# The first weight chunk loaded behind the first x tile, and its products mixed with the turns of the later tiles

## What is computed

```
z = x @ w_in                       # 1152 x 1024 by 1024 x 6216; columns: q, k, v, qi, ki, wi, xr, gr, ga, gb
q, k, qi, ki = rope(...)           # rotary position on the heads
attn = sparse_attention(...)       # an indexer (qi, ki, wi) picks the keys of each query, then softmax
rnn  = RG-LRU(conv(xr)) * gelu(gr) # needs softplus(-lru_lambda), gate biases, conv weights: "the vectors"
x = LayerNorm1(alpha * x + (sigmoid(ga) * (attn @ w_a) + sigmoid(gb) * (rnn @ w_r)) @ w_out)
x = LayerNorm2(alpha * x + HierMoE(x))
```

## Time and profile before

| | |
|---|---|
| median of 3 runs | 1666.08 us (1664.17 to 1671.99) |
| the profiled execution, its own time | 1661.35 us |
| its span | 1659.5 us |
| mean granted TensorE clock | 0.956 of full speed |
| busy in the span: TensorE / VectorE / ScalarE / GpSimd | 1496.0 / 876.7 / 531.9 / 434.4 us |

### The profile page before, as it was taken

The page is one execution under the profiler, slowest core; times in us unless marked ns, Lnnn a source line. Parts: engine busy times, 40 slices in busy tenths (PEclk is TensorE's granted clock), DMA queues, the critical chain, the costliest instruction groups (busy, mean ns, idle before and its releaser), DMA issues.

```text
span 1659.5 us, 24972 instructions
## 1 busy us (share of the span) xinstructions
PE 1496.0 (90%) x10014; PEld 1344.0 (81%) x10014; DVE 876.7 (53%) x1648; ACT 531.9 (32%) x960; POOL 434.4 (26%) x465
## 2 busy tenths in 40 slices
PE   5989999999999899899999998999994299999990
PEld 5976679899999567789899897999994288888880
DVE  4025827999996577431546465443265034434445
ACT  4224542211111565520465655011011022222225
POOL 0744534813233000013334343231100302111110
PEclk7999999999999899999999999999998599999995
DMA  5111010232232830853111111244015768888946
GB/s 190 37 30 29 26 45 16 66 114 82 81 105 72 247 87 25 314 178 91 35 46 42 45 36 47 88 170 150 30 77 200 277 209 228 247 249 277 265 120 247
DMA packets 138089, 204.08 MB, mean 123 GB/s; under 512 B 14676, under 2 KB 89396, under 8 KB 137984
## 3 DMA queue, kind: packets, MB, share of 16 engines
q1 hardware_dynamic: 131808, 180.53, 33.6%
q0 software_dynamic: 6176, 22.10, 5.6%
HBM read 143.99 MB, written 58.61 MB: 122 GB/s over the span
## 4 chain that ended last, share of the span: by engine, by line
PE 76%; DMA 10%; DVE 5%; POOL 4%; issue 2%; ACT 2%; SPq 1%; POOLq 0%; DVEq 0%; ACTq 0%
PE psum L544 18%; PE psum L546 17%; PE psum L545 17%; DMA w_gate_up<-in_w_gate_up 5%; PE psum L1326 5%; PE psum L1140 3%; DMA x_and_experts_by_token<-expert_out,row_token 2%; PE psum L1130 2%; PE psum L1009 2%; PE psum L1162 2%; PE psum L1111 2%; POOL x_by_expert L935 1%; PE psum L1278 1%; PE psum L1318 1%; POOL roped L899 1%
## 5 line engine op out<-in xcount | busy, mean ns | idle before, releaser
L544 PE MATMUL psum<-x_hi,ring_hi 128*128 128x384 f32 x768 | 259.0, 337 | 0.5 <-ACT v L1518 0.5
L546 PE MATMUL psum<-x_lo,ring_hi 128*128 128x384 f32 x768 | 256.6, 334 | 0.0
L545 PE MATMUL psum<-x_hi,ring_lo 128*128 128x384 f32 x768 | 256.5, 334 | 0.0
L905 POOL CAST ring_hi<-ring_raw 128x512 fp32r<-128x512 f32 x88 | 67.1, 763 | 582.3 <-PE psum L546 415.8
L1326 PE MATMUL psum<-expert_rows_T,w_gate_up 128*128 128x192 f32 x1024 | 176.4, 333 | 13.2 <-DMA w_gate_up<-in_w_gate_up 11.8
L1326 PEld LDWEIGHTS psum<-expert_rows_T,w_gate_up 128*128 128x128 f32 x1024 | 171.9, 195 | 17.5 <-issue 8.4
L544 PE MATMUL psum<-w_hi,x_hi 128*128 128x256 f32 x576 | 174.0, 302 | 6.5 <-DVE channel_vectors L1781 3.7
L545 PE MATMUL psum<-w_hi,x_lo 128*128 128x256 f32 x576 | 165.3, 287 | 0.0
L546 PE MATMUL psum<-w_lo,x_hi 128*128 128x256 f32 x576 | 165.1, 287 | 0.0
L544 PEld LDWEIGHTS psum<-x_hi,ring_hi 128*128 128x128 f32 x768 | 144.2, 188 | 1.7 <-ACT v L1518 0.7
L545 PEld LDWEIGHTS psum<-x_hi,ring_lo 128*128 128x128 f32 x768 | 144.2, 188 | 1.1
(11 more groups left out here) (335 smaller groups left out, 3039.3 us busy)
## 6 DMA issues: line engine op xcount, KB each, us to landing
w_gate_up<-in_w_gate_up SPq DMA_DIRECT2D x16, 2048.0 KB, 14.1
ring_raw<-in_w_in SPq DMA_DIRECT2D x64, 256.0 KB, 3.4
w_down<-in_w_down SPq DMA_DIRECT2D x16, 1024.0 KB, 7.5
expert_rows<-x_by_expert SPq DMA_DIRECT2D x16, 774.0 KB, 5.5
x_by_expert<-zeros SPq DMA_DIRECT2D x7, 1536.0 KB, 16.2
gate_sigmoid<-sigmoid_out SPq DMA_DIRECT2D x15, 576.0 KB, 3.2
w_raw<-in_w_in SPq DMA_DIRECT2D x16, 512.0 KB, 4.4
k_cache<-in_cache_k SPq DMA_DIRECT2D x8, 1024.0 KB, 6.0
```

What stands on the lines that cost most here:

```text
L544: nc.tensor.matmul(out, ah, bh, start=first, stop=False)
L545: nc.tensor.matmul(out, al, bh, start=False, stop=False)
L546: return nc.tensor.matmul(out, ah, bl, start=False, stop=last)
L905: link(g.tensor_copy(RHI[:, p_ % 2, :, :], RRAW[:, p_ % 2, :, :]))
```

## The change

Chunk 0 is loaded right behind x tile 0. TensorE turns tiles 0, 1 and 2, and then turns tile t+2 ahead of product (0, t) for t = 1 to 6; a product of chunk 0 waits for the low parts of its own tile alone. The turns of x use PSUM banks 4 to 7 instead of 0 to 3. ScalarE splits chunk 0 behind the high parts of tile 0, and VectorE behind the low parts of tile 0; the other tiles' parts follow in the order of the turns. The rotary table is loaded behind x tile 4, under the semaphore of the small constants; the vectors and the router biases are loaded behind tile 8, and chunk 1 behind them. The vectors are turned (bank 6) ahead of the last product of chunk 0, and `kw_products` waits for their copy. ScalarE splits chunk 1 in the steps (0,5) and (0,6) and runs its softplus ahead of the result of (1,3); VectorE makes the low parts of chunk 1 ahead of the vectors, and those of chunks 2 and 3 behind the softplus. GpSimd clears `WQ` at once.

```diff
+    def x_before(t):
+        return range(3) if t == 0 else range(t + 2, min(t + 3, TT))
...
                 sp.dma_start(XIN[:, t % 3, :], x_rows(t)).then_inc(s_x_loaded[t % 3], 16)
+                if t == 0:
+                    load_chunk(0)
                 if t == 4:
-                    load_chunk(0)
-                    r = 0
-                    for name, n in rows:
-                        sp.dma_start(VIN[r:r + n, :], I[name]).then_inc(s_const, 16)
-                        r += n
-                    sp.dma_start(ROPE[:, :, :], I["c_rope"]).then_inc(s_const, 16)
-                    sp.dma_start(RBIAS[:, 0:4], I["b_router_group"].broadcast_to([128, 4])).then_inc(s_const, 16)
-                    sp.dma_start(RBIAS[:, 4:20], I["b_router_expert"].broadcast_to([128, 16])).then_inc(s_const, 16)
+                    sp.dma_start(ROPE[:, :, :], I["c_rope"]).then_inc(s_misc, 16)
+            r = 0
+            for name, n in rows:
+                sp.dma_start(VIN[r:r + n, :], I[name]).then_inc(s_const, 16)
+                r += n
+            sp.dma_start(RBIAS[:, 0:4], I["b_router_group"].broadcast_to([128, 4])).then_inc(s_const, 16)
+            sp.dma_start(RBIAS[:, 4:20], I["b_router_expert"].broadcast_to([128, 16])).then_inc(s_const, 16)
...
-            pool.wait_ge(s_x_lo, XT0)
-            pool.wait_ge(s_vectors_ready, 1)
             g.memset(WQ[:, :, :], 0.0).then_inc(s_setup, 1)
...
-                        pool.wait_ge(s_const, 16 * 10)
+                        pool.wait_ge(s_misc, 16 * 2)
...
-            for t in range(TT):
+            def turn_x(t):
+                pe.wait_ge(s_x_loaded[t % 3], 16 * (t // 3 + 1))
                 for hf in range(2):
                     i = 2 * t + hf
                     wait(pe, s_x_lo, i - 3)
                     for k in range(4):
-                        last = tr(PS[:, i % 4, 128 * k:128 * k + 128],
+                        last = tr(PS[:, 4 + i % 4, 128 * k:128 * k + 128],
...
-            pe.wait_ge(s_const, 16 * 10)
+            def turn_vectors():
+                pe.wait_ge(s_const, 16 * 9)
+                pe.wait_ge(s_x_lo, XT0)
                 for k in range(KB):
-                    last = tr(PS[:, 4, NV * k:NV * k + NV], VIN[0:NV, 128 * k:128 * k + 128], IDENT[0:NV, 0:NV])
+                    last = tr(PS[:, 6, NV * k:NV * k + NV], VIN[0:NV, 128 * k:128 * k + 128], IDENT[0:NV, 0:NV])
-            pe.wait_ge(s_x_lo, XT0)
-            pe.wait_ge(s_vectors_ready, 1)
...
             def kw_products():
+                pe.wait_ge(s_vectors_ready, 1)
...
+                if c == 0:
+                    for tile in x_before(t):
+                        turn_x(tile)
+                    if t == TT - 1:
+                        turn_vectors()
+                    pe.wait_ge(s_x_lo, 2 * t + 2)
                 if t == 0:
                     pe.wait_ge(s_chunk_lo, 2 * (c + 1))
...
+                    if c == 0:
+                        for tile in x_before(t):
+                            high_x(tile)
+                            if tile == 0:
+                                high_chunk(0, 0)
+                                high_chunk(0, 1)
+                        if t in (5, 6):
+                            high_chunk(1, t - 5)
+                    if gi == POS[1, 3]:
+                        softplus()
...
-                    if t in (0, 3) and c + 1 < NCH and c != C_KW:
+                    if t in (0, 3) and 1 < c + 1 < NCH and c != C_KW:
                         high_chunk(c + 1, t // 3)
...
+                if i == 1:
+                    low_chunk(0)
-            low_chunk(0)
+            low_chunk(1)
             dve.wait_ge(s_vectors_turned, 1)
...
-            for c in range(1, DVE_SPLITS):
+            for c in range(2, DVE_SPLITS):
                 low_chunk(c)
```

More of the change, by code:

```diff
@@ L962, in _ @@
             pe.wait_ge(s_misc, 16)
-            for t in range(TT):
+            def turn_x(t):
+                pe.wait_ge(s_x_loaded[t % 3], 16 * (t // 3 + 1))
                 for hf in range(2):
                     i = 2 * t + hf
-                    if hf == 0:
-                        pe.wait_ge(s_x_loaded[t % 3], 16 * (t // 3 + 1))
                     wait(pe, s_x_lo, i - 3)
                     for k in range(4):
-                        last = tr(PS[:, i % 4, 128 * k:128 * k + 128],
+                        last = tr(PS[:, 4 + i % 4, 128 * k:128 * k + 128],
                                   XIN[:, t % 3, 128 * (4 * hf + k):128 * (4 * hf + k) + 128], IDENT)
                     last.then_inc(s_x_transposed, 1)
-            pe.wait_ge(s_const, 16 * 10)
-            for k in range(KB):
-                last = tr(PS[:, 4, NV * k:NV * k + NV], VIN[0:NV, 128 * k:128 * k + 128], IDENT[0:NV, 0:NV])
-            last.then_inc(s_vectors_turned, 1)
-            pe.wait_ge(s_x_lo, XT0)
-            pe.wait_ge(s_vectors_ready, 1)
+            def turn_vectors():
+                pe.wait_ge(s_const, 16 * 9)
+                pe.wait_ge(s_x_lo, XT0)
+                for k in range(KB):
+                    last = tr(PS[:, 6, NV * k:NV * k + NV], VIN[0:NV, 128 * k:128 * k + 128], IDENT[0:NV, 0:NV])
+                last.then_inc(s_vectors_turned, 1)
             def transpose_group(gi):
@@ L1420, in high_chunk, with high_x, softplus @@
                 a_(WH[:, c % 2, ks, 0:w], WRAW[:, half, :, 0:w], ACT.Copy).then_inc(s_chunk_hi, 1)
[L1422 to L1435, removed]
+            def high_x(t):
+                for hf in range(2):
+                    i = 2 * t + hf
+                    act.wait_ge(s_x_transposed, i + 1)
+                    a_(XH[:, 4 * hf:4 * hf + 4, 128 * t:128 * t + 128],
+                       PS[:, 4 + i % 4, :].rearrange("p (k n) -> p k n", k=4), ACT.Copy).then_inc(s_x_hi, 1)
+            def softplus():
+                act.wait_ge(s_vectors_ready, 1)
+                lam = VEC[:, :, 7]
+                link(a_(VTMP[:, 0, :], lam, ACT.Abs))
+                a_(VTMP[:, 1, :], VTMP[:, 0, :], ACT.Exp, scale=-1.0).then_inc(s_softplus_act, 1)
+                act.wait_ge(s_softplus_dve, 1)
+                a_(VTMP[:, 7, :], VTMP[:, 2, :], ACT.Ln).then_inc(s_softplus_act, 1)
             def store_turned(gi):
@@ L1493, in sample_index_step @@
                        scale=HD ** -0.5).then_inc(s_smp_relu, 1)
-            act.wait_ge(s_x_lo, XT0)
             for gi in range(NG + 2):
@@ L1776, in _ @@
                 ks, ts = slice(4 * hf, 4 * hf + 4), slice(128 * t, 128 * t + 128)
-                v.tensor_tensor(XL[:, ks, ts], PS[:, i % 4, :].rearrange("p (k n) -> p k n", k=4),
+                v.tensor_tensor(XL[:, ks, ts], PS[:, 4 + i % 4, :].rearrange("p (k n) -> p k n", k=4),
                                 XH[:, ks, ts].bitcast(f32), ALU.subtract).then_inc(s_x_lo, 1)
-            low_chunk(0)
+                if i == 1:
+                    low_chunk(0)
+            low_chunk(1)
             dve.wait_ge(s_vectors_turned, 1)
-            v.tensor_copy(VEC[:, :, :], PS[:, 4, 0:KB * NV].rearrange("p (k n) -> p k n", k=KB)).then_inc(s_vectors_ready, 1)
+            v.tensor_copy(VEC[:, :, :], PS[:, 6, 0:KB * NV].rearrange("p (k n) -> p k n", k=KB)).then_inc(s_vectors_ready, 1)
             dve.wait_ge(s_vectors_ready, 1)
```

## The result

| | before | after |
|---|---|---|
| median, runs side by side | 1668.36 us (4 runs, 1664.17 to 1671.99) | 1646.38 us (4 runs, 1644.79 to 1651.5) |
| ratio after / before | | 0.9874 [0.984, 0.9909] |
| profiled execution, its own time | 1661.35 us | 1644.79 us |
| its span | 1659.5 us | 1643.0 us |
| mean granted TensorE clock | 0.956 | 0.963 |

What follows compares the result with a forecast made beforehand. TensorE's work plus its idle places bound the kernel. First product at 15.5, plus 29.56 for products and 6.4 for turns, gave 51.5 instead of 62.22 us; a gain of 11 from the median 1666.08 gave 1655 us, range 1648 to 1662.

Steps and rivals of the forecast that it cites:

- step 1: Head, loads and turns up to the first product: it starts at 15.5 us instead of 32.66.
- step 2: The nine products of chunk 0: 29.56 us, kept as before, the first at half clock.
- the spread of a median: Measured time: a microsecond or two of spread, included in the range of 1648 to 1662 us.
- the pieces said to cost nothing: Moved loads, splits, softplus and clearing: covered by slack elsewhere, such as ScalarE's 2.43 us idle per step; cost nothing.
- slow bound: Head loads: four later pieces at 2.6 us each, tile 2 landing at 15.9, first product at 17.5 us.
- The lower bound: Head loads: five 512 KB pieces at 302 GB/s land at 11 us, first product at 12.5.
- Rival A: Better head: loads at the mean rate, first product at 12.5 us, clock full; 16.7 us less, 1649.4; chance 0.15.
- Step 3: Turns of tiles 3 to 8 and of the vectors, now inside chunk 0's products: 6.4 us added, bounds 5.6 and 7.2.
- the forecast: Head: ninth product of chunk 0 ends at 51.5 us instead of 62.22; case of gains 8.3 to 14 us, chance 0.62.
- B: Head gain mostly lost: slow loads and turns, one more half-clock product; 5.8 us less, 1660.3; chance 0.16.
- C: Slower: half clock through all of chunk 0, ending 12.8 us later than 62.22, or 1679 us; chance 0.04.
- D: Behind the head: something later starts on its own clock, so the gain misses the end; 1666 us; chance 0.03.

Runs made afterwards that it cites:

- the repeats: The changed kernel run again twice without an edit, beside the kernel before: 1650.6 us (ratio 0.9921) and 1651.24 us (ratio 0.9925).

## Why the prediction was right and wrong

**Direction and mechanism: right; three terms of the sum: mis-sized.** These are the pace of the landings (step 1), the first product at half clock (step 2) and the spread of a median. The head was TensorE waiting for loads in an order that served nothing; the change took that away, every moved piece stayed hidden, and the rest of the kernel passed the gain on unchanged. The softplus chain, moved to (1,3), was one of the pieces said to cost nothing. ScalarE's timeline after:

```profile
56.31 0.22 ACT L1447 ACTIVATE vec_tmp<-channel_vectors 128x8 f32<-128x8 f32 x1
...
56.79 1.28 ACT L1450 ACT_TABLE_LOAD   x1
...
58.20 0.43 ACT L1433 ACTIVATE w_hi<-w_raw 128x288 fp32r<-128x288 f32 x1
```

It ended at 58.3, the following result came on time (55.77, then 58.86, a step of 3.09 as before). Chunk 1 was issued at 28.2 (34 allowed), its last low part was begun at 39.4 and wanted at 46.5; no turn inside the chunk waited on a load.

**Step 1, the first product: too late by 2.5 us.** It said 15.5; it was 12.99, and 13.2 and 13.75 in the repeats. The failed term is the pace of landings, 2.3 us for a half and 1.9 for a tile, 8.4 us for four pieces. The five pieces landed at 4.7, 6.9, 8.4, 9.8 and 11.0 us, 1.2 to 2.2 apart and 6.2 us for the last four (6.2 and 6.5 in the repeats). Another 0.8 us is tile 0, which landed earlier than in before (5.5); in the repeats it landed at 5.4 and 4.7. Against these 3.0 us stands the turn of tile 2, which ended 2.0 us behind its landing and not 1.6, since it had to wait for tile 1's at the slow pace. The time from issue to landing, of tile 0 (issued at 1.19), of the two halves (1.65, 2.12) and of tiles 1 and 2 (2.67, 3.23):

```profile
DMA to landing us min/median/max: 3.6/3.6/3.6
DMA to landing us min/median/max: 5.3/5.8/6.3
DMA to landing us min/median/max: 7.1/7.4/7.7
```

That time grows from piece to piece, while the distance between two landings stays below 2.3 us. The prediction took its 2.3 (and the 2.6 of its slow bound) from times of this kind, with no working from them; no row showed the distance of two landings of a half. The lower bound, from the mean rate, was the nearer one: it had the last piece at 11 us.

**Step 2, the products: "with the first at half clock as now" failed in the first trace.** It took 3.16 us instead of 5.25, 2.1 us less. In the repeats it took 3.8 and 4.2, so the term is not a constant but lies between 3.1 and 5.5 (the second trace of before) by the moment at which the pace doubles. Rival A argued for a full clock, and the prediction against it, from the record's 1.00 from 5.6 to 16 us, as something that a pause could take away. It was no measurement: tile 0's eight transposes took 1.94 us there, the slow pace, so there was no full clock to lose, and the question was when it would first come. It came after 12.8 us in the first trace, after 15.2 and 15.5 in the repeats and after 16.5 with two tiles first; why at one time and not another is open. With extra transposes the product took 3.1 to 3.2 us in all three kernels that had them; so it did in two that had none, the early chunk alone and all tiles turned first.

**Step 3, turns inside the chunk: right.** 6.4 us was said, 6.0 is what is left: 46.49 - 12.99 = 33.50, less 3.16 for product 0 and 24.3 for the other eight. Together 2.5 + 2.1 + 0.4 = 5.0 us, from 51.5 to 46.49. The 2.1 is in part luck, since the repeats got 1.5 and 1.1 of it. This is rival A, given 0.15, in the first trace (its 9th result would come at 45.5), and something between A and the forecast in the repeats.

**The step from trace to median.** "A microsecond or two of spread of a median" was too small. The tail behind the head moves by 6 to 7 us between traces of one kernel, and medians of the kernel before lie between 1662.69 and 1668.36. The median after lies 19.7 us below the 1666.08 that the sum started from. Of these, 16.5 are seen in the spans; 3.2 come from where the profiled executions lie, 4.7 us below the median before and 1.6 below the median after, which the sum took to be the same. With the two sizes above, that carried the median out of the range; both repeats lie inside it, at 1650.6 and 1651.2.

**Rivals B, C and D** did not come. B needed slow landings and one more product at half clock: the landings were faster than forecast, and in no trace did a second product of chunk 0 run at half clock, not even where the first took 4.4 and 5.1 us (chunk behind tile 2, and two tiles first, 9th at 48.4). C's half clock through the chunk never appeared in any kernel. D: the stretches behind kept their length.

## What to carry to other kernels

Sum the start of a kernel from landing-to-landing times of queued pieces, not from the issue-to-landing time of one. Where the first work is short and waits between loads, count its instructions per microsecond before believing the clock record, and price the first big product at both levels. When a part is measured alone, split its gain into the earlier start and the pace of what follows (1.4 and 2.1 us for the early chunk here), and do not take the whole for the sum of such parts: how much a part is worth hangs on the others, and a difference under 0.5% wants a repeat of the same kernel beside it.

## What was not expected of the hardware

The record of the granted clock reads 1.00 until its first change, while sixteen transposes take 3.44 us and eight later ones 1.04. Transposes alone raise the clock (0.25 us each, then 0.118), and with 28 of them in idle places of the head product 0 took 3.1 to 3.2 us in three traces of three; but the moment of the rise still moved between them, from 6.4 to 10.4 us, and where it came late the extra transposes held up the next turn. With four waits of up to 2.2 us on GpSimd's rotated tiles, 8.8 us together in each of the traces compared, the same stretch took 35.4 us at 0.95 in one execution and 39.3 us at 0.83 in another; with the waits filled the clock stayed at 1.00. The expert stretch took 284.3 to 295.4 us over the traces with no edit near it; what sets it was not tried.
